# Sample attention: two key groups turned one behind the other, behind every second convolution product

## The reference

```python
# sample attention: keys at strides 1, 4 and 16 from a cache of 2048 rows
kg = k_all[:, idx]
vg = v_all[:, idx]
s = jnp.einsum('bthc,btkhc->bthk', q, kg)
s = s * (HEAD_DIM ** -0.5) + bias.T[None, None]
p = jax.nn.softmax(s, axis=-1)
return jnp.einsum('bthk,btkhc->bthc', p, vg)

# convolution group
u = gc * hc
conv = conv_w[0] * u_ext[:, 0:T]
for j in range(1, CONV_WIDTH):
    conv = conv + conv_w[j] * u_ext[:, j:j + T]
y_conv = gb * conv
```

## Time and profile before

| | |
|---|---|
| time, median of 3 runs | 1083.86 us (1081.44 to 1083.96) |
| the profiled execution, time | 1085.75 us |
| the profiled execution, span from first to last instruction | 1083.9 us |
| mean granted clock of TensorE | 0.981 |
| busy: PE, DVE, ACT, POOL | 1038.5, 509.9, 296.1, 156.2 us |

### The profile page before, as it was taken

One profiled execution on the slowest core, in us unless ns is written; L12 is line 12 of the kernel. 1 busy time (PEld: TensorE's weight loads), 2 busy tenths in 40 slices (PEclk: granted clock), 3 DMA queues, 4 the chain that ended last, 5 costly groups with the idle time before them and its releaser, 6 DMA issues.

```text
span 1083.9 us, 15520 instructions
## 1 busy us (share of the span) xinstructions
PE 1038.5 (96%) x5834; PEld 619.9 (57%) x5834; DVE 509.9 (47%) x1201; ACT 296.1 (27%) x621; POOL 156.2 (14%) x171
## 2 busy tenths in 40 slices
PE   5999999899999999999999998989999998899997
PEld 4888876565878777766555553334433333345443
DVE  4836535778644454434556565341111110047674
ACT  2332322777322321101111123111111111144331
POOL 0000001024500020003011112222231111130000
PEclk9999999999999999999999999989999998999999
DMA  9724123860753555454873227989999999874321
GB/s 321 192 78 146 44 89 112 263 174 14 262 175 98 176 175 173 156 185 155 347 278 120 94 95 279 391 348 415 417 410 409 421 419 400 348 287 173 128 78 77
DMA packets 103435, 241.84 MB, mean 223 GB/s; under 512 B 20390, under 2 KB 61262, under 8 KB 88832
## 3 DMA queue, kind: packets, MB, share of 16 engines
q1 hardware_dynamic: 92720, 211.83, 54.0%
q0 software_dynamic: 9920, 26.38, 6.4%
q10 hardware_dynamic: 720, 2.62, 0.6%
HBM read 206.84 MB, written 38.67 MB: 227 GB/s over the span
## 4 chain that ended last, share of the span: by engine, by line
PE 89%; DMA 4%; DVE 4%; ACT 1%; issue 1%; SPq 0%; POOL 0%; POOLq 0%; DVEq 0%; ACTq 0%
PE pair L2855 14%; PE pair L2545 13%; PE pair L3074 13%; PE pair L2926 11%; PE pair L3178 7%; PE pair L3096 6%; PE pair L3173 3%; PE pair L2679 2%; DMA R<-in_w_up 2%; PE pair L2653 2%; PE pair L2694 2%; PE pair L3061 1%; PE pair L2756 1%; PE pair L2773 1%; PE pair L3153 1%
## 5 line engine op out<-in xcount | busy, mean ns | idle before, releaser
L2855 PE MATMUL pair<-R 128*128 128x264 f32 x672 | 160.4, 389 | 0.0
L3074 PE MATMUL pair<-R 128*32 128x512 f32 (+2 forms) x896 | 154.5, 613 | 4.0 <-DVE R L2273 2.2
L2545 PE MATMUL pair<-R 128*128 128x256 f32 x672 | 150.2, 383 | 3.2 <-DVE R L1647 3.2
L2545 PEld LDWEIGHTS pair<-R 128*128 128x128 f32 x672 | 127.6, 192 | 21.8 <-DVE R L1647 3.8
L2855 PEld LDWEIGHTS pair<-R 128*128 128x128 f32 x672 | 123.5, 190 | 23.0 <-issue 4.4
L2926 PE MATMUL pair<-R 128*128 128x512 f32 x256 | 118.3, 614 | 0.0
L2278 DVE TENSOR_TENSOR R<-pair,R 128x256 f32<-128x256 f32 x21 | 8.9, 425 | 210.8 <-ACT R L1460 210.8
L3074 PEld LDWEIGHTS pair<-R 128*32 128x32 f32 (+2 forms) x896 | 49.3, 127 | 93.8 <-issue 89.2
L3096 PE MATMUL pair<-R,bias 128*32 128x512 f32 (+2 forms) x448 | 77.6, 608 | 3.1 <-issue 2.6
L2926 PEld LDWEIGHTS pair<-R 128*128 128x128 f32 x256 | 48.2, 195 | 54.4 <-issue 53.7
L3178 PE MATMUL pair<-R 128*128 128x512 f32 x168 | 73.0, 593 | 0.0
(11 more groups left out here) (373 smaller groups left out, 1420.0 us busy)
## 6 DMA issues: line engine op xcount, KB each, us to landing
R<-in_w_gate SPq DMA_DIRECT2D x32, 1024.0 KB, 12.7
R<-in_w_up SPq DMA_DIRECT2D x32, 1024.0 KB, 16.1
R<-in_w_down SPq DMA_DIRECT2D x32, 1024.0 KB, 17.3
R<-in_x_prompt SPq DMA_DIRECT2D x16, 512.0 KB, 3.9
R<-in_cache_k SPq DMA_DIRECT2D x8, 1024.0 KB, 5.1
R<-in_cache_v SPq DMA_DIRECT2D x8, 1024.0 KB, 4.9
R<-y_dram SPq DMA_DIRECT2D x16, 512.0 KB, 5.6
R<-in_w_in SPq DMA_DIRECT2D x15, 512.0 KB, 6.8
```

Source lines behind the costliest of these rows:

```text
L2545: last = mm(qbank(p, part, k), lhs[:, c, :], rhs[:, c, :], start=(c == 0), stop=(c == 3))
L2855: last = mm(cbank(u, chain), w[:, c, :], xq[:, x, c, j, :], start=(c == 0 and n in (0, 1, 3)), stop=(c == 3), skip_group_check=True)
L3074: last = mm(bk[2 + u][r, :].rearrange("p (w f) -> p w f", w=2), xgT[u][:, c, r], wgu[s][:, :, c, :], start=(c == 0), stop=(c == DC - 1))
```

## The change

Both groups of a key part are turned one directly behind the other, behind products 1, 3 and 5, where only the first group stood. Nothing stands behind products 0, 2, 4 and 6 any more. The same is done in the lists of ACT and DVE. In DVE's list the second far copy thus comes ahead of `taps` (product 0), of `join_lower` and `conv_sums` (product 4), and ahead of `lower_out`; in ACT's list the second near copy of a part behind product 1 comes ahead of the copy of product 2. No instruction is added or dropped, and no semaphore's counts change.

```diff
--- before.py
+++ after.py
@@ -1359,14 +1359,12 @@
         for u in range(UNITS):
             k = 3 * u
             keep_product(u, 0)
-            if u >= 1:
-                second_keys(*SAMPLE_PARTS[k - 1])
             if u == 1:
                 act.wait_ge(S("ssa"), 2)
                 root(ra[:, 0:PT], ssa[:, 0:PT], AD).then_inc(S("ra_root"), 1)
             sample_part(*SAMPLE_PARTS[k])
+            second_keys(*SAMPLE_PARTS[k])
             keep_product(u, 1)
-            second_keys(*SAMPLE_PARTS[k])
             if u == 6:
                 square_y(0)
                 square_y(1)
@@ -1374,6 +1372,7 @@
             sample_part(*SAMPLE_PARTS[k + 1])
             second_keys(*SAMPLE_PARTS[k + 1])
             sample_part(*SAMPLE_PARTS[k + 2])
+            second_keys(*SAMPLE_PARTS[k + 2])
         square_y(2)
         square_y(3)
         act.wait_ge(S("ssa"), 3)
@@ -2074,13 +2072,14 @@
                 add_squares(0)
                 add_squares(1)
             sample_part(*SAMPLE_PARTS[k + 1])
+            second_keys(*SAMPLE_PARTS[k + 1])
             join_lower(u)
             if u % 2 and u + 1 < UNITS:
                 conv_sums(u // 2 + 1, 1, 3)
-            second_keys(*SAMPLE_PARTS[k + 1])
             join_upper(u)
             upper_out(u)
             sample_part(*SAMPLE_PARTS[k + 2])
+            second_keys(*SAMPLE_PARTS[k + 2])
             lower_out(u)
             if u % 2 and u + 1 < UNITS:
                 conv_sums(u // 2 + 1, 4, 4)
@@ -2877,8 +2876,7 @@
                 conv_product(u, n)
                 if n % 2:
                     sample_part(*SAMPLE_PARTS[k + n // 2])
-                elif k + n // 2 >= 1 and n < 6:
-                    second_keys(*SAMPLE_PARTS[k + n // 2 - 1])
+                    second_keys(*SAMPLE_PARTS[k + n // 2])
                 if u == 0 and n >= 3:
                     head_squares(n - 3)
```

## The result

The changed kernel takes 1097.98 us (median of 4 runs, 1096.25 to 1099.28), against 1083.91 us of the kernel before (4 runs, 1081.44 to 1086.24). The ratio is 1.0119, with a 95% interval of 1.0104 to 1.0134: 12.9 us slower (11.3 to 14.5). The two medians lie 14.1 us apart, inside that interval; the forecast was 1096.8 us.

What follows compares the result with a forecast made beforehand. TensorE, busy 218.08 of 219.00 us, was taken to bound the convolution stage. Terms 10.2 + 1.2 + 0.6 + 1.5 − 0.7, unrounded 12.9 us, on the median 1083.86 gave 1096.8 us, range 1089 to 1106.

Steps and rivals of the forecast that it cites:

- 16 near waits with restart: At each pair's second near group, TensorE waits for ACT's copy of bank 4: 0.59 plus 0.05 us, 10.2 us in all.
- far waits of units 1, 3, 7: Behind product 5, DVE's join and weight sums delay the far copy; TensorE loses 0.41 us each, 1.2 us.
- far wait of unit 4: Behind product 5, three filters behind DVE's join delay the far copy; TensorE loses 0.6 us.
- unit 6, near and far: Behind product 3, ACT's squares and DVE's sum of them delay both copies: 1.5 us beyond the counted near wait.
- the four old waits: TensorE's four earlier waits on DVE's far-key copies lie in pairs and are replaced by the new waits: −0.7 us.
- The product was the cover: Before, the 1.78 us product behind each group hid both bank copies; 16 pairs lose it between their halves.
- the rival of a falling clock: Clock falls to half at the pairs, 1.7 us per fall; 1124 us if at all 16. Chance 0.10.
- Give-back later: In the late expert stage, TensorE's 1.9 us wait for in_w_up absorbs part of the delay: 1094.9 us. Chance 0.09.
- The copies did not stay hidden: Rival: at second groups bank 4 is free in time, only the old waits go: −0.7, 1083.2 us. Chance 0.04.

Runs made afterwards that it cites:

- the runs with a half and a quarter of a product: Changed kernel with two (half) or one (quarter) of the next product's four matmuls between a pair's groups; ratio to before 1.0017 and 1.0045.
- four groups in a row: Changed kernel with all four key groups of a sequence in a row, in the place of its second part; ratio to before 1.0165.
- the moved copies: Changed kernel with DVE's first far copies behind product 5 put ahead of join and filters, unit 6's squares behind the copies; ratio to before 1.0093.
- the one with bank 3: Changed kernel with the second near group of six pairs (sequences 1 to 3) put into bank 3 instead of bank 4; ratio to before 1.0112.

## Why the prediction was right

The forecast was 12.9 us slower, and by the ratio 12.9 were measured, by way of the same steps. That the two agree to the tenth is luck: the interval is 11.3 to 14.5, the medians lie 14.1 apart, the stage grew by 13.1. The pairs' losses, each from the first near group to what follows the pair, less 1.52 us (the forecast of the stage is 218.5 + 12.9):

| step | forecast, us | profile after, us |
|---|---|---|
| 16 near waits with restart | 16 × 0.64 = 10.2 | 0.65 to 0.71 each, 11.0 |
| far waits of units 1, 3, 7 | 3 × 0.41 = 1.2 | 0.33, 0.34, 0.38: 1.05 |
| far wait of unit 4 | 0.6 | 0.55 |
| unit 6, near and far | 1.5 | 1.4 |
| the first pair, behind DVE's other work | not counted | 0.1 |
| the four old waits | −0.7 | −0.7 |
| sum | 12.9 | 13.4 |
| growth of the stage | | 13.1 |

- **The product was the cover.** This was the main step, and the runs with a half and a quarter of a product show it: what the work between two groups covers of the copy is given back, and no more.
- **The size of a near wait** was a little too small. The term that was off is the release, the time from the end of a copy to the start of the group that waits for it. I took 0.06 us from a wait on DVE's copy. In the changed kernel's near waits it is 0.14 in the pair of unit 1 (310.39 to 310.53), near the 0.15 of the earlier trace rows, and about 0.10 from unit 6 on. That is 0.8 us in all. It is not ACT's copy as such that makes it longer: with four groups in a row two of three near waits end 0.04 to 0.07 behind the same copy. The third of them belongs to a call of `keys` of its own, and each call begins with a wait for the ring's buffer, ahead of the wait for bank 4; the second groups of the changed kernel have it too. That this extra wait is the reason is argued from the lists: no run takes it away alone. The far waits were 0.3 us too large. The two errors partly cancel. Of the sum of 13.4, 0.3 do not show in the stage's growth.
- **The far waits** came in the five places that were named, and the moved copies took them away.
- **The clock** stayed at 1.00. Unit 6 held TensorE without a product for 3.56 us in the changed kernel, and four groups in a row for 5.1 us, so the rival of a falling clock had its best chance here and did not come. The stretch of unit 6:

```profile
403.10:406.80 3.70, 2.09 (x17) 1.56 (x16) 2.93 (x3) 2.21 (x4) 3.70 (x2) 1.00 0.00 0
```

  The fall that gave this rival its price does not come back each time either. The same small matmuls and the stretch behind them, first in the changed kernel, then in the one with bank 3:

```profile
519.62 1.99 PE L2895 MATMUL pair<-ones,R 128*128 128x1 f32 x18
522.20:525.60 3.40, 3.40 (x10) 1.56 (x9) 2.76 (x11) 0.37 (x2) 1.10 (x2) 1.00 0.05 11
519.86 1.99 PE L2898 MATMUL pair<-ones,R 128*128 128x1 f32 x18
522.60:526.00 3.40, 3.40 (x6) 1.34 (x5) 2.92 (x11) 0.21 (x2) 1.10 (x2) 0.50 0.05 11
```

  Of the eight profiles only those of the kernel before and of the bank 3 run have a fall there. What decides it stays open.
- **Give-back later** did not show. Its place was TensorE's wait for in_w_up, which was to shrink from 1.9 us. In the changed kernel it has grown:

```profile
PE pair L3072 <- DMA R<-in_w_up: 3.0, 2, 1.5
```

  In the experiments it is 1.8 to 3.7 us, and 3.5 where the stage is longest. The growth of the whole by the ratios (12.9, 1.8, 4.9, 10.1, 17.9, 12.2 and −1.1 us, with some 1085 us as the base) differs from the stage's growth by −0.7 to 0.8 us and is nowhere less by 1.9; each figure alone has an interval of 1.5 to 3 us to either side. The time outside the stage in the profiled executions was 865.4 before, 862.6 changed, and 863.1, 863.9, 865.4, 866.6, 866.2 and 867.7 us in the experiments, in the order of the table. It follows no change of the stage. What moves the rest by some 5 us from run to run stays open; falls of the clock such as the one above are part of it in some profiles, but no run set them apart.
- **The copies did not stay hidden**: the single bank gave TensorE nothing to do for 0.45 to 0.51 us of each pair (0.70 in unit 6), as the profile has it. I had named near 0.6 as the sign, and busy time nearly unchanged; the busy time grew by 3.5 us, since the modelled ends of the transposes hide part of each wait. The limit that I gave this rival, a copy of under 0.2 us, was wrong: ACT's copy starts 0.69 after the pair and TensorE wants the bank at 0.76, so even a copy of 0.1 us would have shown.

## What to carry to other kernels

Where one engine fills a single PSUM bank and another empties it, work between two fillings is the cover of the copy: count from the first instruction of a filling to the copy's end and the release (here 1.38 to 1.44 us, unit 6 apart), take off the filling itself and what stands between (0.76 us without the product), and what is left is lost each time on the engine that bounds the stage. Before buying a second bank, look at which wait stands right behind the one that it removes. And an engine that is idle half the time can still be late: what counts is what stands ahead of the copy in its list.

## What the runs showed of the hardware that was not expected

- The near transposes that waited on ACT's copy started 0.04 to 0.07 us after its end where the wait for the bank stood first in TensorE's list, and 0.09 to 0.15 where a wait for the ring's buffer stood ahead of it. Behind DVE's far copies, with the wait for the bank first, it was 0.05 to 0.06.
- Stretches of up to 5.1 us of float32 transposes with waits between them left the granted clock at 1.00. The 2.6 us of one-column and other small matmuls behind the stage came ahead of a fall in two of eight profiles, and the clock stayed at 1.00 in the other six.
